# Moving the head outputs' copies behind the next head's scores, and the low parts of the out weights into the last chunks of the merge

## What is computed

```python
h = x @ w_in[i]
(fq, fk, fv, ff_logit, sq, sk, sv, dq, dk, dv, iq, ik, iw, g) = split_cols(h)
...
o_fox = fox_attention(fq, fk, fv, log_f)                 # 6 heads of 64 channels
o_sb = stick_breaking_attention(sq, sk, sv)              # 5 heads
o_dsa = dsa_attention(dq, dk, dv, iq, ik, iw)            # 5 heads
gates = jax.nn.sigmoid(g.reshape(b, s, N_BRANCH, D_MODEL))
merged = (gates[:, :, 0] * (o_fox @ w_up_fox[i])
          + gates[:, :, 1] * (o_sb @ w_up_sb[i])
          + gates[:, :, 2] * (o_dsa @ w_up_dsa[i]))
x = layer_norm(DEEPNORM_ALPHA * x + merged @ w_out[i], ln1_g[i], ln1_b[i])
ffn = jnp.square(jax.nn.relu(x @ w_ff_in[i])) @ w_ff_out[i]
ple = jax.nn.sigmoid(x @ w_ple_gate[i]) * (p[i] @ w_ple[i])
x = layer_norm(DEEPNORM_ALPHA * x + ffn + ple, ln2_g[i], ln2_b[i])
```

## Time and profile before

| | |
|---|---|
| median of 3 runs | 1537.96 us (1535.28 to 1540.37) |
| the profiled execution's own time | 1535.46 us |
| its span in the trace | 1533.4 us |
| TensorE's mean granted clock in it | 0.978 |
| PE busy | 1454.3 us (95%) |
| DVE busy | 900.1 us (59%) |
| ACT busy | 698.8 us (46%) |

### The profile page before, as it was taken

How to read it: one execution, slowest core, us unless ns; L and a number is a source line. 1 busy time by engine, 2 the same in 40 slices (tenths; PEclk the granted TensorE clock), 3 DMA queues, 4 the chain that set the end, 5 groups by cost and what they waited for, 6 DMA issues and landing times. The chain is left out here.

```text
span 1533.4 us, 25756 instructions
## 1 busy us (share of the span) xinstructions
PE 1454.3 (95%) x10597; PEld 1185.9 (77%) x10597; DVE 900.1 (59%) x1410; ACT 698.8 (46%) x1184; POOL 44.7 (3%) x57
## 2 busy tenths in 40 slices
PE   4999989988999989999999999999999999999996
PEld 2557777656888869998887888878989887788885
DVE  1653343425656555577687656575557769656565
ACT  3232325433444434476743444454457664444443
POOL 0000530000000000000000000000000000000000
PEclk9999999999999999998999999999999999999998
DMA  9721651006455417432435655524733233855520
GB/s 347 272 105 37 231 202 38 2 1 219 171 186 191 138 38 218 165 111 71 150 111 202 241 190 216 186 68 132 200 110 126 96 111 110 329 178 205 196 78 27
DMA packets 121038, 230.14 MB, mean 150 GB/s; under 512 B 20080, under 2 KB 34672, under 8 KB 120176
## 3 DMA queue, kind: packets, MB, share of 16 engines
q1 hardware_dynamic: 118064, 223.80, 41.9%
q10 hardware_dynamic: 2880, 5.01, 1.0%
HBM read 227.76 MB, written 1.05 MB: 149 GB/s over the span
## 5 line engine op out<-in xcount | busy, mean ns | idle before, releaser
L772 DVE TENSOR_TENSOR work_rounded<-ring,work_rounded 128x1024 fp32r<-128x1024 f32 x208 | 240.9, 1221 | 88.3 <-ACT work_rounded L764 88.2
L733 PE MATMUL psum<-channels_rounded,work_rounded 128*128 128x512 f32 x768 | 273.4, 400 | 1.6 <-DVEq L1752 1.3
L746 PE MATMUL psum<-work_rounded 128*128 128x512 f32 x1152 | 266.5, 390 | 0.0
L993 PE MATMUL psum<-channels_rounded,ring_rounded 128*128 128x256 f32 x1728 | 249.1, 285 | 2.7 <-PEq L2935 1.5
L764 ACT ACTIVATE work_rounded<-ring 128x1024 fp32r<-128x1024 f32 x208 | 203.3, 1050 | 106.1 <-PE psum L746 102.6
L746 PEld LDWEIGHTS psum<-work_rounded 128*128 128x128 f32 x1152 | 214.6, 188 | 45.5
L993 PEld LDWEIGHTS psum<-channels_rounded,ring_rounded 128*128 128x128 f32 x1728 | 222.6, 191 | 9.1 <-issue 7.8
L735 PE MATMUL psum<-channels_rounded,work_rounded 128*128 128x256 f32 x768 | 216.2, 281 | 0.0
L733 PEld LDWEIGHTS psum<-channels_rounded,work_rounded 128*128 128x128 f32 x768 | 144.9, 189 | 38.1 <-issue 2.6
L735 PEld LDWEIGHTS psum<-channels_rounded,work_rounded 128*128 128x128 f32 x768 | 145.7, 190 | 0.8
L1498 DVE TENSOR_TENSOR ring_rounded<-ring,ring_rounded 128x1024 fp32r<-128x1024 f32 x80 | 94.1, 1197 | 29.5 <-ACT ring_rounded L1292 28.8
(11 more groups left out here) (366 smaller groups left out, 1997.8 us busy)
## 6 DMA issues: line engine op xcount, KB each, us to landing
ring<-in_w_in SPq DMA_DIRECT2D x20, 2048.0 KB, 8.1
ring<-in_w_ff SPq DMA_DIRECT2D x16, 2048.0 KB, 8.4
ring<-in_w_ff_in SPq DMA_DIRECT2D x16, 2048.0 KB, 8.0
ring<-in_w_ff_out SPq DMA_DIRECT2D x16, 2048.0 KB, 8.0
ring<-in_w_mod SPq DMA_DIRECT2D x12, 2048.0 KB, 9.0
ring<-in_w_out SPq DMA_DIRECT2D x6, 2048.0 KB, 8.3
ring<-in_w_in SPq DMA_DIRECT2D x8, 1024.0 KB, 5.7
ring<-in_w_up SPq DMA_DIRECT2D x4, 2048.0 KB, 8.0
```

Of the source, the lines that this page charges most:

```text
L733: pe.matmul(v3(psum[:, 4 + m, :], SEQ), w1[0][:, k, m * P:(m + 1) * P], y_both[:, :, k, :], start=(k == 0), stop=False, skip_group_check=True)
L746: mm = pe.matmul(psum[:, 2 * t + n, :], h[ph][:, kq, t * P:(t + 1) * P], w2[pw][:, kq, n * 512:(n + 1) * 512], start=False, stop=False, sk ...
L772: dve.tensor_tensor(parts.low[i % 2][:, at], ring[:, SLOT * s + 1024 * c:SLOT * s + 1024 * (c + 1)], exact(parts.high[i % 2][:, at]), ALU. ...
L993: mm = pe.matmul(ps[:, at:at + SEQ], u[pw][:, k, col:col + P], y_parts[py][:, k, :], start=((k, n) == (0, 0)), stop=((k, n) == (KC - 1, 2)))
```

## The change

Three things. The steps of ACT and DVE for `oT` get a name of their own in the schedule, `oT in`. PE's transpositions stay where they were; for `oT0` and `oT1` the copy and the low part come after the new head's scores. The reads of `oT` count on "right" and no longer on "dve". In the merge, DVE's low part of an `out0` piece stands one chunk earlier, and behind `gated_left`; the last one is inside chunk 7.

```diff
         if kind:
             steps.append(("S", f"{kind}{h}"))
+        if n in CHANNELS_AT:
+            steps.append(("oT in", CHANNELS_AT[n]))
...
         if n == len(HEADS) - 1:
-            steps.append(("oT", "2"))
+            steps += [("oT", "2"), ("oT in", "2")]
...
-            steps += [("up", "1a"), ("oT", "3"), ("up", "2a")]
+            steps += [("up", "1a"), ("oT", "3"), ("oT in", "3"), ("up", "2a")]
...
-            j.add(f"oT{n}", "dve", wide=True)
+            j.add(f"oT{n}", "right", wide=True)
...
-                            elif kind == "oT":
+                            elif kind == "oT in":
                                 c = int(name)
                                 act.wait_ge(products_done, j2.full(f"oT{c}"))
...
-                                ps = r.open(f"oT{c}")
+                                ps = right.open(f"oT{c}")
                                 dve.wait_ge(o_high, c + 1)
-                                r.read(f"oT{c}", dve.tensor_tensor(oT_low[c], v3(ps, SEQ),
+                                right.read(f"oT{c}", dve.tensor_tensor(oT_low[c], v3(ps, SEQ),
                                                                    exact(oT_high[:, 2 * c:2 * c + 2, :]), ALU.subtract))
...
                         for c in range(KC):
                             if c < 4:
                                 low("up1", c)
-                            elif c > 4:
-                                low("out0", c - 5)
                             if c:
                                 gated_left(c)
+                            if c > 3:
+                                low("out0", c - 4)
                             ps = right.open(f"up{c}b", SEQ)
...
                         merged_low(KC - 1)
-                        low("out0", 3)
                         low("out1", 0, 1, 2, 3)
```

More of the change, by code:

```diff
@@ L400, in layer_jobs @@
         elif kind == "oT":
-            j.add(f"oT{n}", "dve", wide=True)
-        elif kind != "sigmoid":
+            j.add(f"oT{n}", "right", wide=True)
+        elif kind not in ("sigmoid", "oT in"):
             j.add(f"{kind}_{n}", {"gate": "gate", "rot": "dve", "S": "dve", "V": "dve",
@@ L1138, in _ @@
                         for kind, name in attention_schedule():
-                            if kind == "sigmoid":
+                            if kind in ("sigmoid", "oT in"):
                                 continue
@@ L1604, in _ @@
                             elif kind == "oT":
+                                pass
+                            elif kind == "oT in":
                                 c = int(name)
-                                ps = r.open(f"oT{c}")
+                                ps = right.open(f"oT{c}")
                                 dve.wait_ge(o_high, c + 1)
-                                r.read(f"oT{c}", dve.tensor_tensor(oT_low[c], v3(ps, SEQ),
+                                right.read(f"oT{c}", dve.tensor_tensor(oT_low[c], v3(ps, SEQ),
                                                                    exact(oT_high[:, 2 * c:2 * c + 2, :]), ALU.subtract))
```

## The result

The changed kernel takes 1543.88 us (1543.46 to 1547.4, 6 runs) against 1538.68 us (1535.28 to 1540.37, 6 runs): the ratio is 1.0044 with a 95% interval of 1.0031 to 1.0056, or 4.8 to 8.6 us more. The times given are medians and the ratio is one of means (1544.85 to 1538.06), which is why it says +6.8 us where the medians differ by 5.2. Measured again beside its two halves it was 1.0027 (1.0014 to 1.0039). Both say slower; together they give 1.0035, 5.4 us.

A forecast was written before the change was run, and what follows sets the result against it. DVE was taken to set the pace of the merge and first layer norm. Terms +6.1 (merge), +1.6 (clock), -0.7 (heads) and -0.2 (count) gave +6.8 us, forecast 1544.5 us, range 1539 to 1550.

The forecast's parts named there:

- The loop in the merge: Merge chunks 4 to 7: DVE's low parts wait for ACT, 4.00 us per chunk against 3.39; +6.1 us in two layers.
- PE's 1.85 us: Out product: PE waits for the merged sum and resumes 1.85 us later than before in each layer.
- The delay is carried into the MLP: Behind the merge: DVE's 3.05 us delay passes through PE in block (1, 1) into the MLP, with nothing taking it up.
- The clock: Ahead of block (1, 1): PE idles 1.4 us, then one fall to the low clock in the two layers, +1.6 us.
- The rival that the stalls are partly taken up: Merge: if DVE is not last, only PE's 1.85 us per layer count; +2.8 us, 1540.8, chance 0.27.
- The heads: Turns 8 on: `lnot` wait shrinks from 1.63 to 0.92 us; first layer -0.7, second 0, plus -0.2 for removed waits.
- the lead is taken back: Dsa heads: PE leads by 0.71 us, but ACT and DVE take that back unless DVE gains too.
- The 0.1 us per removed wait: Low parts of `oT` on DVE: the separate count saves 0.1 us per removed wait, two that matter, -0.2 us.
- my list of PE's waits near the change: Four rows: 4.6 us for out weights' low part, 3.3 for `lnot`, 0.9 and 0.4 for ACT in the dsa heads.

The follow-up runs named there:

- early_high: The changed kernel with ACT's high parts of `out0`, and the first of `out1`, one chunk earlier, DVE's order kept; 0.9988, -1.8 us against before.
- half_loop: The changed kernel with only `out0` pieces 2 and 3 moved up, 0 and 1 at their old place; one profiled execution, merge stages 1.3 us longer each.
- after_copy: The changed kernel measured once more, unaltered, beside its two halves; 1.0027 against before, +4.1 us.
- merge_only: The kernel before with only the merge part of the change, heads as before; 1.0034 against before, +5.2 us.
- early_up1: early_high with the four high parts and first three low parts of `up1` moved ahead of `oT3`; 0.9991 against before, -1.4 us.
- after_ln: The changed kernel with DVE's four low parts of the first MLP weights spread over the first layer norm; 1.0036 against before, +5.5 us.
- before_copy: The kernel before, unaltered, run once more for its trace of the low clock; one execution, no total time given.
- early_ln: early_up1 with DVE's four low parts of the first MLP weights spread over the first layer norm; 1529.66 us, 0.9938 against before.
- heads_only: The kernel before with only the heads part (`oT` steps and count), old merge; 0.9976 against before, -3.7 us.

## Why the prediction was right, and where not

**The loop in the merge: right, in mechanism and size.** Forecast 4.00 us per chunk and 3.05 us per layer, measured 3.98 and 2.95. The idle time marked before each low part is 0.50, since it is counted from the recorded end of L1597, 0.68 us after its start, while in the earlier trace rows the instruction behind L1595 starts 0.60 after it; the period shows the full 0.6. early_high takes the wait away and the loss goes; half_loop halves it. PE's 1.85 us was measured as 1.86. The delay is carried into the MLP as forecast: ahead of block (1, 1)'s residual DVE waits 3.52 and 3.53 us for PE in the two layers, where it was 3.52 and 3.57 (the second in the earlier trace rows).

**The clock: wrong place.** I took one fall ahead of block (1, 1), +1.6 us. The step that failed is that PE would stand there for 1.4 us and meet the low clock after it. In the changed kernel's trace the low clock behind the 3.04 us wait lasted twice as long, PE arrived without a wait, and nothing fell. In after_copy's second layer the clock was back sooner, PE did wait 1.51 us for DVE, and the clock did not fall either. In its first layer the clock was not low behind the wait in the out product at all, PE waited 1.94 us, and again it stayed at 2.4 GHz. Its rows follow, first those of the second layer, then that of the first with its stretch (columns as in the earlier trace rows):

```profile
1290.41 2.90 PE L1212 MATMUL psum<-ring_rounded,work_rounded 128*128 128x512 f32 x6 [3.03 <-DVE work_rounded L1684]
...
1306.04 1.29 PE L1014 MATMUL psum<-shared_consts,x_tok 128*128 128x128 f32 x8 [1.51 <-DVE x_tok L1733]
```

```profile
819.20 1.29 PE L1014 MATMUL psum<-shared_consts,x_tok 128*128 128x128 f32 x8 [1.94 <-DVE x_tok L1733]
```

```profile
819.00:823.00 4.00, 3.77 (x20) 3.11 (x21) 3.45 (x7) 1.21 (x2) 0.00 (x0) 1.00 0.02 4
```

The Trainium skill's section on the HAM clock gate (TensorE: Matmul & The Clock Gate), as I applied it, made every longer pause a risk; that last step was my inference, and the traces don't bear it out. There was no fall behind the pause of 1.51 us, behind two of 1.94 (here and in merge_only's first layer) and behind early_up1's 2.92, while the 1.63 us wait for `lnot` was followed by one every time, and so was early_high's 1.94 us in the out product (a low clock of 3.4 us in both layers). The length of a pause alone does not tell; what does is open. In all these passes of the whole change the stage is the same, 74.4 and 74.5 us in the first layer and 51.5 twice in the second: DVE's delay stands as a floor, and PE's low clock lies under it. The term was 0. The whole came out at +6.8 and +4.1 all the same, beside +6.8 in the sum; that the first agrees to the digit is luck. Without that term the sum is +5.2, near the mean of +5.4.

**The rival that the stalls are partly taken up** fell for a reason I had not seen. after_ln removes DVE as the last, and PE by itself is as late, through the longer low clock. It had that low clock of 6.8 us in both layers of its trace. Of the ten passes with a wait of 3.03 to 3.05 us in the out product seven have it, one has 3.4 us and two none. What the spreading would give in passes like the last three is not shown.

**The heads: right that the lead is taken back.** In turn 9 the wait for `lnot` is 1.21 us (forecast 0.9). The chain did get the 0.7 us shorter: from PE's T of one head to its T of the next it is 10.32 us before (698.29 to 708.61) and 9.59 after (706.83 to 716.42). Some 0.2 us of that came out of a wait ahead of V that no row marks: V starts 5.94 us behind the start of the gates before, 5.71 after. Behind the wait for `lnot` the clock stays at 2.4 GHz in the changed kernel, so PE comes earlier to every later turn, and finds the chain of DVE and ACT where it was:

```profile
716.42 0.67 PE L1168 MATMUL psum<-work,shared_consts 128*128 128x256 f32 x2 [1.21 <-DVE work L1637]
...
722.62 0.41 PE L1189 MATMUL psum<-work 128*128 128x64 f32 x2 [0.23 <-DVE work L1666]
...
725.41 0.67 PE L1168 MATMUL psum<-work,shared_consts 128*128 128x256 f32 x2 [1.49 <-DVE work L1637]
...
734.15 0.67 PE L1168 MATMUL psum<-work,shared_consts 128*128 128x256 f32 x2 [0.36 <-DVE work L1637]
...
739.95 0.41 PE L1189 MATMUL psum<-work 128*128 128x64 f32 x2 [0.84 <-DVE work L1666]
```

The three rows of L1168, and three alike in the second layer, are the six waits on the page. They are not new losses: PE had spent the same time at half speed. This is why the spared low clock is worth so little. Nor is the low clock always spared: in 7 of the 18 passes with the new heads one stands behind one of the waits in the heads, in six of them for 3.4 us.

Forecast -0.9 for both layers. Without the chance fall the first layer has 92.2 to 92.3 against 92.4 (with it 95.3 against 96.2), and the second 90.6 to 92.5 against 90.8 to 94.7. The means over all traces differ by 0.7 and 0.9, 1.6 in all; without the traces with the chance fall in the first layer, and without before_copy's 94.7 in the second, it is about 0.5. The times gave -3.7 (-5.5 to -1.7), -2.3 (-4.5 to 0) and, in early_ln, -0.3. That the heads' part gains is shown by the first of these, and that the low clock gets rarer by the mean granted clock over all runs, 0.9825 in heads_only against 0.978. How much of it reaches the end stays open. The sign of this term is right; its size, -0.9, lies outside the first interval and inside the second.

The 0.1 us per removed wait can be read at `oT2`, which has the same instruction behind it in every kernel, the reciprocal (L1673, after the change L1677). With the old count it starts 0.72 to 0.73 us behind L1608, with the new one 0.61, in both layers of every trace, five with the old count and nine with the new. Here it is in the first layer, before and after:

```profile
761.39 0.69 DVE L1608 TENSOR_TENSOR work_rounded<-psum,work_rounded 128x512 fp32r<-128x512 f32 x1 [3.60 <-ACT work_rounded L1415]
762.11 0.17 DVE L1673 RECIPROCAL small<-small 128x2 f32<-128x2 f32 x1
```

```profile
768.95 0.69 DVE L1612 TENSOR_TENSOR work_rounded<-psum,work_rounded 128x512 fp32r<-128x512 f32 x1 [3.61 <-ACT work_rounded L1417]
769.56 0.15 DVE L1677 RECIPROCAL small<-small 128x2 f32<-128x2 f32 x1
```

So the term is real on DVE; whether it reaches the end of the kernel is not shown.

I also left out a row in my list of PE's waits near the change, which I called four:

```profile
PE psum L1105 <- DVE work_rounded L1608: 4.8, 2, 2.4
```

It is the wait for the low part of `oT2`. The change leaves it at 4.8, but the chance fall behind it is what makes the heads hard to read.

## What to carry over

Moving a consumer one step earlier is free only if its producer moves too: look at what the producer itself waits for, and if that is the consumer's own engine, the two form a loop whose length is the new period. Before shortening one engine's path, work out the second one's: here spreading DVE's work alone gave 0.4 to 0.5 us per layer (on the changed kernel), taking away PE's pause alone gave 1.8 us in one layer and lost 1.0 in the other, and both together gave 4.8 to 4.9.

## What the hardware showed that I had not expected

The same pause is followed by a low clock of different length in different executions. After the 3.03 to 3.05 us wait in the out product it lasted 6 to 7 us in the changed kernel's trace in both layers, but in after_copy the first layer shows none and the second half as much. merge_only shows none in the first layer and 6.8 us in the second. After the 2.42 us wait it is 6.8 us, 3.4 us (in the second layer alone) or nothing. Each such fall moves PE by up to 3 us, so one trace against another can be off by as much as the change is worth; the stages with the same state of the clock agree to 0.2 us.
